# A decoder trunk with gathered experts: the order of steps in the expert stages, and of two instructions on GpSimd

## The reference

```python
for l in range(2):
    h = _rmsnorm(x, norm_mix_g[l])
    z = h @ w_in[l]                      # 2072 columns: queries, keys, values, gates, conv and pool inputs
    x = x + concat([o_nsa, o_conv, o_pool]) @ w_out[l]
    x = x + _cross_attention(_rmsnorm(x, norm_xa_g[l]), _rmsnorm(mem, norm_mem_g[l]), ...)
    x = x + _peer(_rmsnorm(x, norm_ffn_g[l]), peer_wq[l], peer_subkeys[l], peer_u[l], peer_v[l])
return _rmsnorm(x, final_g)
```

## Time and profile before

| | |
|---|---|
| median of 3 runs | 1901.41 us (1895.86 to 1905.76) |
| profiled execution, its own time | 1897.98 us |
| its span (first to last instruction) | 1896.2 us |
| busy, DVE / PE / POOL / ACT | 1133.7 / 1375.9 / 677.6 / 514.9 us |
| moved by DMA | 702.57 MB |
| granted TensorE clock, mean | 0.852 |

### The profile page before, as it was taken

One profiled execution on the slowest core, in us unless ns is written; L12 is line 12 of the kernel. 1 busy time (PEld: TensorE's weight loads), 2 busy tenths in 40 slices (PEclk: granted clock), 3 DMA queues, 4 the chain that ended last, 5 costly groups with the idle time before them and its releaser, 6 DMA issues. The chain is left out here.

```text
span 1896.2 us, 23075 instructions
## 1 busy us (share of the span) xinstructions
PE 1375.9 (73%) x8428; PEld 714.3 (38%) x8428; DVE 1133.7 (60%) x2788; ACT 514.9 (27%) x1311; POOL 677.6 (36%) x1028
## 2 busy tenths in 40 slices
PE   6899956767889983946878863957878874555554
PEld 4666752234554551412444631422444631111110
DVE  5431359876342477689743567688743579864444
ACT  3331122154221222223522222223522221211111
POOL 0000025433333352534433351434433354555551
PEclk9899978889899996977989895977989887777776
DMA  7434589998999999999999998999999999999996
GB/s 272 178 151 178 199 355 399 423 422 353 364 364 399 371 422 409 371 422 403 421 415 397 395 420 346 379 422 400 421 413 397 390 421 371 404 423 421 421 421 268
DMA packets 87380, 702.57 MB, mean 371 GB/s; under 512 B 9952, under 2 KB 10080, under 8 KB 12128
## 3 DMA queue, kind: packets, MB, share of 16 engines
q0 software_dynamic: 73728, 536.90, 68.9%
q1 hardware_dynamic: 13536, 164.15, 21.9%
HBM read 698.92 MB, written 2.10 MB: 370 GB/s over the span
## 5 line engine op out<-in xcount | busy, mean ns | idle before, releaser
L1154 PE MATMUL acc_pe<-uv_rows,diag 64*64 64x512 f32 x4096 | 622.1, 741 | 346.4 <-ACT diag L908 338.0
L461 DVE CUSTOM_DVE_ANT_0 uv_rows<-uv_rows,h_ps 128x1024 f32<-128x1024 f32 x512 | 603.0, 1218 | 196.4 <-DMA uv_rows<-uv_in,idx 191.5
L426 POOL TENSOR_TENSOR diag<-ident_st,gate 128x64 f32<-128x64 f32 x512 | 167.4, 327 | 1097.5 <-PE acc_pe L1154 832.9
L429 POOL DMA_INDIRECT uv_rows<-uv_in,idx x512 | 510.1, 996 | 84.3 <-issue 51.2
L1154 PEld LDWEIGHTS acc_pe<-uv_rows,diag 64*64 64x64 f32 x4096 | 160.3, 158 | 726.6 <-ACT diag L908 501.1
L902 ACT ACTIVATE gelu_b<-act_b 128x2 f32<-128x2 f32 x256 | 51.9, 203 | 901.5 <-DVE act_b L461 891.1
L1181 PE MATMUL bank<-h_t,w_ring 128*128 128x128 f32 x1792 | 210.5, 279 | 11.3 <-DMA w_ring<-blocks_in 9.1
L1181 PEld LDWEIGHTS bank<-h_t,w_ring 128*128 128x128 f32 x1792 | 205.8, 195 | 31.8 <-issue 29.0
L1181 PE MATMUL bank<-w_ring,h_t 128*128 128x512 f32 x448 | 201.0, 603 | 3.0 <-ACTq L944 3.0
L908 ACT ACTIVATE diag<-diag,gelu_b 128x64 f32<-128x64 f32 x512 | 150.2, 340 | 8.4
L1181 PEld LDWEIGHTS bank<-w_ring,h_t 128*128 128x128 f32 x448 | 84.2, 193 | 119.5 <-issue 115.6
(11 more groups left out here) (200 smaller groups left out, 1173.9 us busy)
## 6 DMA issues: line engine op xcount, KB each, us to landing
w_ring<-blocks_in SPq DMA_DIRECT2D x72, 2048.0 KB
uv_rows<-uv_in,idx POOLq DMA_INDIRECT x512
tcon<-tile_consts_in SPq DMA_DIRECT2D x4, 656.5 KB, 13.0
smalls<-smalls_in SPq DMA_DIRECT2D x3, 816.5 KB, 8.5
h_ffn<-ffn_gain_in SPq DMA_DIRECT2D x4, 512.0 KB
xs<-x_in SPq DMA_DIRECT2D x2, 512.0 KB, 10.6
uv_rows<-mem_in SPq DMA_DIRECT2D x1, 1024.0 KB, 16.3
mem_gained<-uv_rows SPq DMA_DIRECT2D x1, 1024.0 KB, 4.8
```

Of the source, the lines that this page charges most:

```text
L426: nc.gpsimd.tensor_tensor(diag[:, slot_of(k), :], ident_st[:, :], gate[:, k:k + 1].to_broadcast([P, HT]), ALU.mult).then_inc(sems["gates_s ...
L429: nc.gpsimd.indirect_dma_start(uv_rows[:, slot_of(k), :, :].rearrange("p a n -> p (a n)"), None, a["uv"], bass.IndirectOffsetOnAxis(ap=idx ...
L461: v.tensor_tensor_reduce(u_row, u_row, h_ps[:, :], 1.0, 0.0, ALU.mult, ALU.add, act_b[:, k // B % AHEAD, k % B:k % B + 1]).then_inc(sems[" ...
L1154: mm = pe.matmul(acc_pe[c * HT:(c + 1) * HT, r * BLK:(r + 1) * BLK], diag[tok, slot_of(k), :], uv_rows[tok, slot_of(k), 1, c * BLK:(c + 1) ...
```

## The change

Three things change. `PLAN` and `MEM_PLAN` get a new order, `LENGTH` and `spread` deal out the batches otherwise (one batch is run in the step `start`, before any step of the plan; TensorE and ScalarE do theirs after the first step), and in `gather` the indirect DMA is issued ahead of the diagonal. No arithmetic is added or removed. Of the table one line of each is shown:

```diff
-PLAN = ["rank1", "rank_pairs1", "look_up1", "gates1", "rank2", "mix_norm", "zq", "ab", "rank_pairs2", "gates2",
+PLAN = ["mix_norm", "zq", "rank1", "ab", "rank_pairs1", "look_up1", "conv_in", "gates1", "zk1", "rank2",
...
-LENGTH = {"mix_norm": 6, "ab": 8, "zq": 8, "zk1": 8, "zk2": 8, "conv_in": 3, "conv": 4, "rope": 3, "branch_gates": 2,
+LENGTH = {"mix_norm": 4, "ab": 4, "zq": 4, "zk1": 4, "zk2": 4, "conv_in": 0, "conv": 4, "rope": 3, "branch_gates": 0,
...
 LAG = 1
+AT_START = 1
...
-    vector, tensor, done, passed = {}, {}, 0, 0
+    vector, tensor, done, passed = {"start": AT_START}, {}, 0, 0
...
-    return {"vector": vector, "scalar": vector, "tensor": tensor}
+    scalar = {**vector, "start": 0, plan[0]: vector[plan[0]] + AT_START}
+    tensor[plan[0]] += AT_START
+    return {"vector": vector, "scalar": scalar, "tensor": tensor}
...
                     def gather(k):
 
-                        nc.gpsimd.tensor_tensor(diag[:, slot_of(k), :], ident_st[:, :],
-                                                gate[:, k:k + 1].to_broadcast([P, HT]), ALU.mult).then_inc(
-                                                    sems["gates_spread"], 1)
                         nc.gpsimd.indirect_dma_start(
                             uv_rows[:, slot_of(k), :, :].rearrange("p a n -> p (a n)"), None, a["uv"],
                             bass.IndirectOffsetOnAxis(ap=idx[:, k:k + 1].bitcast(U32), axis=0)).then_inc(
                                 landed[slot_of(k)], 16)
+                        nc.gpsimd.tensor_tensor(diag[:, slot_of(k), :], ident_st[:, :],
+                                                gate[:, k:k + 1].to_broadcast([P, HT]), ALU.mult).then_inc(
+                                                    sems["gates_spread"], 1)
```

More of the change, by code:

```diff
@@ L100 @@
 BANKS = 4
-PLAN = ["rank1", "rank_pairs1", "look_up1", "gates1", "rank2", "mix_norm", "zq", "ab", "rank_pairs2", "gates2",
[L105 to L117, removed]
[4 rows of a table removed]
+PLAN = ["mix_norm", "zq", "rank1", "ab", "rank_pairs1", "look_up1", "conv_in", "gates1", "zk1", "rank2",
+        "rank_pairs2", "look_up2", "zk2", "rope", "rank3", "turn_kv", "rank_pairs3", "branch_gates", "gates2", "gates3",
+        "look_up3", "cmp_in", "cmp_hidden", "cmp_hidden_turn", "conv0", "cmp_kv", "conv1", "cmp_scores", "sel_scores",
+        "cmp_probs", "conv2", "cmp_out", "sel_turn", "win_scores", "conv3", "sel_out", "conv_norm", "win_turn",
+        "conv_act", "conv_silu", "win_out", "small_branches", "mix_turn", "wo0", "wo1", "xa_norm", "xq0", "xq1",
+        "xa_scores", "xa_turn", "xa_out", "xo0", "xo1", "ffn_norm", "pq0", "sub_scores0", "rank0", "pq1", "pq2",
+        "sub_scores1", "rank_pairs0", "pq3", "sub_scores2", "look_up0", "gates0", "sub_scores3"]
@@ new lines @@
+MEM_PLAN = ["mix_norm", "zq", "rank1", "ab", "rank_pairs1", "look_up1", "conv_in", "gates1", "zk1", "rank2",
+            "rank_pairs2", "look_up2", "zk2", "rope", "rank3", "turn_kv", "rank_pairs3", "branch_gates", "gates2",
+            "gates3", "look_up3", "cmp_in", "cmp_hidden", "cmp_hidden_turn", "conv0", "cmp_kv", "conv1", "cmp_scores",
+            "sel_scores", "cmp_probs", "conv2", "cmp_out", "sel_turn", "win_scores", "conv3", "sel_out", "conv_norm",
+            "win_turn", "conv_act", "conv_silu", "win_out", "small_branches", "mix_turn", "wo0", "wo1", "xa_norm",
+            "xq0", "xq1", "xa_scores", "xa_turn", "xa_out", "xo0", "mem_kv0", "mem_kv1", "mem_kv2", "mem_kv3",
+            "mem_kv4", "mem_kv5", "xo1", "mem_kv6", "mem_kv7", "ffn_norm", "pq0", "sub_scores0", "rank0", "pq1", "pq2",
+            "sub_scores1", "sub_scores2", "rank_pairs0", "gates0", "look_up0", "pq3", "sub_scores3"]
```

## The result

The changed kernel took 1868.26 us (median of 4 runs, 1864.39 to 1872.43) against 1900.83 us before (4 runs, 1895.86 to 1905.76): a ratio of 0.9834, 95% interval 0.9807 to 0.9862. The same kernel was measured again later (change_again): 0.9807 (0.9785 to 0.9829). One kernel further down, conv0_early, had two executions of six that were far slower (1932.55 and 4359.81 us); its time is the median of the other four. The forecast, 1884 us in 1872 to 1900, had the sign and half of the size: 17 us predicted, 33 measured. No rival of the prediction reached so low either; the lowest, (d), stood at 1877 us. The profiled execution took 1864.39 us where before had 1897.98.

What follows compares the result with a forecast made beforehand. DMA was taken as the bound, full at 421 GB/s. Span: 1896.2 - 21.2 + 3 + 2 - 1 = 1879.0 us, 1880.8 with the 1.8 around it; ratio 0.991 gave 1884 us, 1872 to 1900 for 8 in 10.

Steps and rivals of the forecast that it cites:

- (d): Rival: spread losses at 450 to 510 and 1410 to 1500 us shrink too, by 7 us; 1877 us, chance 0.14.
- the 75 us: DMA losses of the stages against 421 GB/s, without the unavoidable tail: about all that a new order can win.
- The starts: Stages 2, 3 and last: leading with norm and first batch fills the DMA holes; 21.2 us gained, bounds 0 and 24.2.
- Stage 1: First stage with experts: already led with the norm behind one ranking, so no gain was given.
- The middle: End of routing to mix_turn: three more batches and about 31 taps on VectorE; 3 us lost, bounds 0 and 21.5.
- (a): Rival: VectorE frees slots late between routing and mix_turn, so the won time is lost again; 1902 us, chance 0.18.
- (b): Rival: between routing and mix_turn, batches' chains queue behind tap steps of 5.5 us on VectorE; slower, 1916 us, chance 0.08.
- gates0 later: Ends of the loop body: gates some 5.3 us later delay the prefetch; 2 us lost in all, bounds 0 and 10.6.
- The exchange: Gather ahead of diagonal on GpSimd: each gather with a just freed slot 0.45 us earlier; 1 us gained, bounds 0 and 10.
- Rival (c): Stage starts: the first projection waits for its block and the hole stays at half; 1895 us, chance 0.08.
- Rival (e): look_ups among more gathers slow GpSimd's prefetch issues through SBUF interfaces shared with VectorE; 1890 us, chance 0.03.

Runs made afterwards that it cites:

- conv0_early: gates0_early with conv0's tap step moved back behind rope, so one fewer tap step in the middle; 1866.7 us, 0.9835 of before.
- start_zero: The changed kernel without the batch at the very start of a stage (AT_START = 0), the norm still leading; 0.9913 of before.
- norm_lead_alone: The kernel before with only mix_norm and zq moved ahead of rank1 in both plans, old lengths kept; 0.9969 of before.
- gates0_early: The changed kernel with the diagonal ahead of the gather again and gates0 two batches earlier in the loop body; 1861.09 us, 0.9790 of before.
- late_more: gates0_early with 2 more in the lengths of wo, xq, xo and mem_kv; 1859.77 us, 0.9797 of before.
- gather_first_alone: The kernel before with one edit, the gather issued ahead of the diagonal; 1904.12 us, 1.0031 of before.
- order_alone: The changed kernel with the diagonal ahead of the gather again; 1863.04 us, 0.9821 of before.

## Why the prediction was right in sign and short by half

*The method held.* Time is bytes plus losses: the losses of the stages fell by 32.6 us, the span by 33.7. What failed was the share of the 75 us that I thought could be won: two terms, stage 1 at nothing and the middle at a cost of 3 us, were gains.

*The starts* (forecast -21.2): the losses of the first 60 us fell from 25.9 to 4.3, so -21.6. Two of the times held: h ready 7.6 us after the copy (1130.2; forecast 6.9), first slots 10.0 (10.8). The ring request did not: 25.6 us after the copy, forecast 15.8. The prediction read the 7.43 us at 1185.90 as two projections and took half for the first. It is one, zq: the eight matmuls of a batch stand in the timeline as x16, and so do zq's eight. `ab` came only at 1196.86. The missing half (3.7 us), the wait for the block (4.94) and the lower clock (1.8) make up the difference. So that the term's size came out to 0.4 us is in part luck. But the argument gave the norm too much: "nothing hangs on" the block's landing was wrong. Without the batch ahead of it, all batches hang on it, and 23.1 us are lost (start_zero). The batch that I treated as company to the norm carries over 80% of this term at the changed kernel; in the old kernel, where four batches follow the first projection, the early norm alone takes 14.4 of the 25.9 us away (norm_lead_alone).

*Stage 1* (forecast "I give it nothing"): -9.2. This is the step that failed, together with the next. I looked at the order of the first steps and saw the norm already near the front, and did not ask what the new numbers of batches do to the 14.1 us that my own rows showed at 450 to 510. At the same distance from the stage's start the changed kernel loses 7.0 us, and at the place of 1410 to 1500 in stage 3 it loses 1.5 in place of 7.5:

```profile
452.14:512.14 60.00, 51.86 (x313) 30.82 (x310) 20.72 (x38) 15.61 (x38) 20.13 (x32) 0.93 0.94 372
...
1393.00:1483.00 90.00, 77.59 (x532) 46.53 (x528) 46.27 (x105) 26.31 (x70) 35.27 (x55) 0.94 1.00 414
```

*The middle* (forecast +3, bounds 0 to 21.5): a gain was shut out, and came. The loop stages lost 4.5 us less at 60 to 170 and 3.4 less between 170 and the last 20 us. I counted VectorE's work against the traffic of the stretch that gained batches, and not what more batches win in a piece that runs dry. In stage 1 this is shown: one batch more behind mix_turn (34 for 33), among steps that leave up to 28 us between two dots, went with 5.7 us less lost there, and 36 batches with 3.1 us lost in all. In the loop stages the three batches went to the stretch ahead of mix_turn, 28 stand behind it as before, and the 7.9 us took both edits: the new lengths alone won late and lost at 60 to 170 us, the new order alone the other way round (the table of the pieces above). This was rival (d), given 0.14 and 7 us; its two windows won 13.1 us, and stage 1 and both parts of the loop together 17.1. DVE at 75% busy and the DMA share of 1.01 in the middle of stage 3 refute rivals (a) and (b). (The upper bound of this term counts the loop's traffic as 100 us, where 411 GB/s give 97.6; with that it is 5.4 us and not 3 in each loop stage.)

*gates0 later* (forecast +2): right in mechanism, 4.0 us later against the last dot (forecast 5.3), and too small: 5.0 us of loss (3.9 lost in change_again in place of 5.2), which gates0_early takes away. 1 us for each end assumed that the gathers in flight cover the gap.

*The exchange* (forecast -1): the bounds "0 and 10" excluded a loss, and alone it lost 5.5 us (1.0031). In the changed kernel no effect can be told (0.9821 without it, 0.9834 and 0.9807 with it).

*Rival (c)* came as 4.94 us on PE, with at most 1.7 us lost at that start behind the early batch. *Rival (e)*: a gather issue takes 999 ns on average, 996 before. The Trainium skill's rule on GpSimd's and VectorE's common SBUF interfaces (GPSIMD Engine Reference, Key points) changes nothing that can be measured here; by the trace the extra issue time is 1.4 us in all.

*The chances*: the forecast with (d), (e) and all of (c) adds up to 0.74, so the 8 in 10 for 1872 to 1900 needed a part of (a) that the text does not name.

The sum with measured terms: -21.6 (starts), -9.2 (stage 1), -4.5 + 1.1 (60 to 170, loop and last stage), -3.4 (late), +5.0 (ends) is -32.6; 1.1 us of the span's 33.7 is not in these pieces (stage 1 begins 2.1 us later, the last stage's tail is shorter).

**Open:** which of the moved steps lets the new order do with fewer early batches; why leading with the norm costs stage 1 10.9 us in the old plan; why the first stage with experts starts between 258.3 and 262.4 us in kernels that hardly differ ahead of it (258.3 and 261.3 in before and norm_lead_alone, which do not differ there at all); and what the exchange costs on the old kernel.

## What to carry to other kernels

Where a kernel is bound by DMA, sum the idle bandwidth piece by piece, and for each dry piece name the streams that could fill it and what frees each one. An early norm without a batch ahead of the first projection fed one stream and starved the other. Where batches are dealt out among steps, order and weights are one decision: over the three stages each alone won nothing. Count how many batches each piece of a stage gets before and after: in stage 1 the number behind mix_turn told the late loss, and what was added there was missing early (late_more). After such a retune, look at the last step whose output the next stage's prefetch needs: it had slipped, and putting it back closed the gap there, though no gain in time could be told apart.

## What the runs showed of the hardware

With a GpSimd instruction of 0.3 us behind the last gather of a stage, and the program's wait for it, the next stage began 1.7 us after that gather (gather_first_alone, the change); with the instruction ahead of the gather it was 0.2 us (before, order_alone).

In start_zero a weight block was asked for 4.4 us ahead of stage 3 (1131.91). The ten gathers of the prefetch had been issued just before it (10.5 MB by their share of the bytes: 536.90 MB over 512), and so had two smaller loads of SyncE. PE waited for the block until 16 us after the stage's start (1136.32 to 1152.77). In these 20.9 us the DMA engines moved 421 GB/s, 8.8 MB, where the block has 2.1 MB: with the DMA engines full, the early request did not arrive early.
